# Starting rounds of the attention items inside a two-directional scan: (2, 8, 13, 20) becomes (1, 7, 12, 18)

## The chip, the cores and the metric

The kernel runs on one core of a Trainium2 chip. The metric is device time in microseconds (us) of one execution, lower is better. The engines that matter here are TensorE (PE, with its weight loads PEld), VectorE (DVE), ScalarE (ACT), GpSimd (POOL) and SyncE (SP), which issues most DMAs.

## The reference, cut to what matters

The program is two blocks of a model in a row. Each of the two layers of the first block computes, for 1040 tokens, a latent attention of 4 heads and a gated linear recurrence of 8 heads that runs forwards and backwards; both read the same projection and do not depend on each other. Their outputs are concatenated, projected, normalised, and sent through a mixture of experts. The second block (differential attention, gated MLP, feed-forward) comes after and is not touched.

```
y_att = _mla(c_q, c_kv, k_pe, ...)            # softmax(q k^T) v, 4 heads
y_f = _wkv_scan(rh, decay, kd, vh, kk, a, reverse=False)   # S = S*w - sa*b + v*k, step by step
y_b = _wkv_scan(rh, decay, kd, vh, kk, a, reverse=True)
mixed = concatenate([y_att, y_rwkv]) @ w_out[li]
```

## The kernel before, in words

All five engines run an instruction order written out by hand; semaphores tie them together, and each engine takes its instructions strictly as they are written.

**The scan.** In each layer the recurrence is cut into 10 steps of 104 tokens for each direction d (0 forwards, 1 backwards). A step is 32 phases in 23 rounds (`PHASES`, `STEPS` = 23). Direction 1 runs 11 rounds behind direction 0 (`STAGGER`), so that while one direction prepares a step the other solves and puts out its own. A round is numbered 0 to 22 after direction 0. Direction 0 is in phases 0 to 2 in round 0, 3 to 5 in round 1, 6 to 10 in round 2, 11 in round 3, 12 in round 4, 13 and 14 in round 5, 15 in round 6, and then one phase a round; direction 1 does the same from round 11 on. I call round 0 to 10 the first half of a step (direction 0 prepares) and round 11 to 22 the second half (direction 1 prepares).

- Phase 0 is a product with `u` on PE (tiles `u,w` and `u,a`). Phases 1 to 10 are element-wise work: DVE takes the product out of PSUM, ACT does two tanh, DVE a prefix sum (L1542) and the differences (L1548, L1555), ACT three exponentials (L1486, L1488, L1491: `ei`, `eK`, `ea`) and four scalings (L1495), DVE the scaled keys (L1568 `kr`, L1564 `hb`, L1571).
- Phase 11 transposes on PE (`consts,u`, `consts,hb`); it waits for `kr` of L1568. ACT takes the result out as `vT` (L1475), and phase 12 on PE waits for that. Phase 13 waits for L1580 on DVE, which takes phase 12 out.
- Phases 16 to 25 are five levels of a triangular inverse, each with two PE blocks (`T,lm`, then `XX,T` and `T,XX`); after each block DVE (L1600, L1608), and after the second one ACT too, must empty the bank before the next block of the same direction can start. Phases 26 to 31 put out the state and the outputs (`S,kr`, `rh,T`, `vT,hbT` and others).

**The attention** of a layer is 40 items (4 heads by 10 tiles of 104 tokens) in the first layer and 32 (4 by 8 tiles of 128) in the second. An item takes six rounds, k = 0 to 5:

- k = 0: PE, two thirds of the scores (10 matmuls, `kn,qn` and `kpe,...`); k = 1: PE, the last third (5 matmuls), and on DVE the row maximum (L1826 three times, L1829, L1831)
- k = 2: ACT, three exponentials with sums (L1811); SP loads the query of the item after the next one
- k = 3: PE, nine transposes (`consts,p`), and DVE (L1843) and ACT (L1798) copies of them
- k = 4: PE, the product with the values (`v,pT`, 18 matmuls)
- k = 5: DVE scales the output (L1851), ACT squares it (L1815), SP stores it

In every round each engine's order is: one direction, then the attention, then the other direction. The direction in phases 0 to 11 (its first four rounds) always comes last; else direction 0 comes first.

**Where an item begins** is what the change touches. `item_starts` takes four rounds a step (`STARTS`) in the first layer, and in steps 0 and 5 of the second; the other steps of the second layer take three (`FEWER`). The first place is left out in step 0. Nothing else in the schedule moves.

Of the kernel before, what the change touches and what calls it, by code (L numbers as in the profile page):

```python
# [1675 lines left out]

STARTS = (2, 8, 13, 20)
FEWER = (2, 9, 17)  # L1680


def item_starts(li):

    made = []
    for q in range(NT + 1):
        places = STARTS if li == 0 or q in (0, 5) else FEWER
        made += [STEPS * q + at for at in places if q or at != STARTS[0]]
    return made[:4 * TILES_OF[li]]
# [2700 lines left out]
```

## Time and profile before

| what | value |
|---|---|
| median of three runs | 4875.96 us (4870.5 to 4881.09) |
| the profiled execution | 4875.28 us, its span 4873.4 us |
| mean granted clock of TensorE | 0.959 |
| busy over the span | PE 91%, PEld 78%, DVE 64%, ACT 44%, POOL 24% |
| scan and attention of the first layer | 357.0 to 1097.7 us: 740.7 us |
| scan and attention of the second layer | 2174.6 to 2896.9 us: 722.3 us |

The profile is of one execution. Times in it count from the first instruction. A row of the timeline gives start, length, engine, line, operation, tiles and number of instructions, and in brackets the idle time before and what ended it. A helper issues most matmuls, so their line is L291; the tiles tell them apart. A row of the windows gives start and end, length, then for PE, PEld, DVE, ACT and POOL the busy time and the number of instructions, then TensorE's granted clock, the share of DMA time and GB/s. The start of one block on PE to the start of the next is what the block costs PE, since the last matmul of a block still drains while the next ones run.

### The profile page before, as it was taken

What the parts mean: (1) busy time and instruction counts of PE and PEld (TensorE: products, weight loads), DVE (VectorE), ACT (ScalarE), POOL (GpSimd) and SP (SyncE); (2) the same over time, 40 slices, a digit from 0 to 9 for tenths busy, and PEclk for the clock granted to TensorE, in tenths of its full rate; (3) what the DMA queues carried; (4) which work ended last, traced back from release to release, by engine and by line L of the source; (5) the groups of instructions that cost most, each with busy time, mean ns of one, the idle gap of its engine ahead of it and who ended that gap; (6) DMA issues with size and microseconds to landing.
All of it is one profiled execution on the core that took longest, in us unless ns stands there. A gap on an engine that the chain in (4) does not pass through costs nothing. (4 is left out here: it accounts for less than half of the span.)

```text
span 4873.4 us, 125669 instructions
## 1 busy us (share of the span) xinstructions
PE 4442.5 (91%) x55312; PEld 3786.9 (78%) x55312; DVE 3123.6 (64%) x4912; ACT 2158.3 (44%) x3962; POOL 1189.3 (24%) x863
## 2 busy tenths in 40 slices
PE   6989999989799969989989889899979979999999
PEld 6888888886588858878888877688857657888887
DVE  5436666669698874346666677898864475661752
ACT  2333444442388852434434341688743252331431
POOL 1003222322244520012322221444321001222221
PEclk9999999999799989999999999899989799999999
DMA  5411111133367664311111132576651003333332
GB/s 149 144 52 37 39 23 34 25 86 86 135 260 265 252 204 121 114 55 28 36 36 24 24 112 88 223 260 260 239 181 35 9 8 123 95 103 114 116 113 91
DMA packets 378339, 535.76 MB, mean 110 GB/s; under 512 B 117501, under 2 KB 301885, under 8 KB 349749
## 3 DMA queue, kind: packets, MB, share of 16 engines
q1 hardware_dynamic: 335701, 488.54, 30.9%
q0 software_dynamic: 40752, 33.95, 2.3%
q8 instruction: 439, 7.19, 0.6%
q10 hardware_dynamic: 1344, 5.24, 0.3%
q14 instruction: 103, 0.84, 0.1%
HBM read 569.43 MB, written 121.40 MB: 142 GB/s over the span
## 5 line engine op out<-in xcount | busy, mean ns | idle before, releaser
L291 PE MATMUL ps<-w_hi,xbT 128*128 128x512 f32 x1520 | 499.9, 400 | 19.7 <-DVE w L2839 19.7
L291 PE MATMUL ps<-hT,w_in 128*128 128x416 f32 (+1 forms) x2736 | 496.2, 340 | 4.1 <-DVE hT L3126 4.1
L291 PEld LDWEIGHTS ps<-hT,w_in 128*128 128x128 f32 x2736 | 459.9, 196 | 30.3 <-issue 19.4
L2839 DVE TENSOR_TENSOR w<-w,w_hi 128x2048 fp32r<-128x2048 f32 x190 | 425.4, 2278 | 2.2 <-ACT w_hi L2796 2.2
L291 PEld LDWEIGHTS ps<-w_hi,xbT 128*128 128x128 f32 x1520 | 289.2, 190 | 87.5 <-DVE w L2839 28.7
L1657 POOL TENSOR_TENSOR lm<-Ab,consts 116x416 f32<-116x416 f32 x240 | 255.5, 1072 | 415.6 <-PE ps L291 245.2
L2796 ACT ACTIVATE w_hi<-w 128x2048 fp32r<-128x2048 f32 x190 | 355.2, 1935 | 0.0
L291 PE MATMUL ps<-w,xbT 128*128 128x512 f32 x760 | 299.3, 394 | 0.0
L2870 DVE TENSOR_TENSOR w<-w,w_hi 128x2048 fp32r<-128x2048 f32 x95 | 221.6, 2333 | 95.5 <-ACT w_hi L2832 95.5
L291 PE MATMUL ps<-w_hi,actT 128*128 128x512 f32 x760 | 250.8, 391 | 4.9 <-DVE actT L2865 4.9
L291 PE MATMUL ps<-x1T,w_gate 128*128 128x512 f32 x1056 | 248.4, 391 | 3.1 <-DVE x1T L3813 1.6
L291 PE MATMUL ps<-x1T,w_up 128*128 128x512 f32 x1056 | 246.5, 389 | 0.0
L291 PE MATMUL ps<-w_down,act 128*128 128x512 f32 x1056 | 241.3, 391 | 3.2 <-POOL w_down L4039 3.2
L1600 DVE TENSOR_TENSOR XX<-ps,consts 116x416 f32<-116x416 f32 x200 | 117.4, 587 | 193.4 <-PE ps L291 193.0
L291 PEld LDWEIGHTS ps<-x1T,w_gate 128*128 128x128 f32 x1056 | 199.4, 189 | 45.3 <-issue 1.9
L291 PEld LDWEIGHTS ps<-w_down,act 128*128 128x128 f32 x1056 | 199.2, 189 | 44.9 <-POOL w_down L4039 3.6
L291 PEld LDWEIGHTS ps<-x1T,w_up 128*128 128x128 f32 x1056 | 198.3, 188 | 41.1
L4030 POOL TENSOR_TENSOR w_up<-w_up,w_up 128x1024 fp32r<-128x1024 f32 x44 | 116.4, 2646 | 459.4 <-ACT w_up L3952 459.4
L291 PE MATMUL ps<-w_out,mixT 128*104 128x512 f32 (+1 forms) x864 | 218.8, 407 | 10.4 <-DVE w_out L2177 5.8
L2785 POOL DMA_INDIRECT t_ys<-yo,slots x95 | 101.3, 1066 | 464.4 <-PE ps L298 374.0
L291 PEld LDWEIGHTS ps<-w_out,mixT 128*104 128x104 f32 (+1 forms) x864 | 152.3, 179 | 67.4 <-DVE w_out L2177 9.5
L794 POOL TENSOR_TENSOR w_in<-w_in,w_in 128x1024 fp32r<-128x1024 f32 x22 | 56.0, 2546 | 604.8 <-ACT w_in L809 604.8
(464 smaller groups left out, 10782.1 us busy)
## 6 DMA issues: line engine op xcount, KB each, us to landing
w<-in_moe_w_dram SPq DMA_DIRECT2D x192, 1024.0 KB, 12.4
w_gate<-in_w_gate_dram SPq DMA_DIRECT2D x44, 512.0 KB, 3.9
w_up<-in_w_up_dram SPq DMA_DIRECT2D x44, 512.0 KB, 3.9
w_down<-in_w_down_dram SPq DMA_DIRECT2D x44, 512.0 KB, 3.6
w_in<-in_w_in_dram SPq DMA_DIRECT2D x36, 512.0 KB, 4.4
w_out<-in_w_out_dram SPq DMA_DIRECT2D x24, 512.0 KB, 7.7
t_h<-x SPq DMA_DIRECT2D x20, 416.0 KB
kn<-t_kn SPq DMA_DIRECT2D x8, 1040.0 KB, 5.2
```

What stands on the lines that cost most here:

```text
L291: made = e.matmul(out, a, b, start=start, stop=stop)
L794: e.tensor_tensor(w.lo, w.x, w.hf, ALU.subtract).then_inc(*count.tick(li, "lo", n))
L1600: e.tensor_tensor(m.XX[0:HP].rearrange("p (k u) t -> p k u t", k=2), both_banks(P, d, 0)[0:HP].rearrange("p k (u t) -> p k u t", t=H), bc( ...
L1657: e.tensor_tensor(m.LM[lv % 2][0:HP], m.ab[0:HP, :, 0, :], bc(m.lmask[0:HP, H * lv:H * lv + H].unsqueeze(1), [HP, 8, H]), ALU.mult).then_i ...
L2785: e.indirect_dma_start(T["ys"], bass.IndirectOffsetOnAxis(P.slots[:, table_column(b - 2):table_column(b - 2) + 1], 0), m.yo[b % 2], None, ...
L2796: e.activation(w.hi, w.x, ACT.Copy).then_inc(*P.c("moe_act").tick(li, "w13", b, k))
L2839: e.tensor_tensor(w.lo, w.x, w.hf, ALU.subtract).then_inc(*P.c("moe_dve").tick(li, "w13", b, k))
L2870: e.tensor_tensor(w.lo, w.x, w.hf, ALU.subtract).then_inc(*dv.tick(li, "w2", b))
L4030: e.tensor_tensor(w.lo, w.x, w.hf, ALU.subtract).then_inc(*po.tick(0, c, "lo", f))
```

## The change

The rounds in which items begin are other ones: each of the four places of a step is one round earlier, the last one two; of the three places, the first is one round earlier, the second two, and the third one later.

```
-STARTS = (2, 8, 13, 20)
-FEWER = (2, 9, 17)
+STARTS = (1, 7, 12, 18)
+FEWER = (1, 7, 18)
```

So with four places PE's attention blocks stand as follows (an item that begins late in a step ends in the next one):

| round | 0 | 1 | 2 | 3 | 4 | 5 | 6 | 7 | 8 | 9 | 10 | 11 | 12 | 13 | 14 | 15 | 16 | 17 | 18 | 19 | 20 | 21 | 22 |
|---|---|---|---|---|---|---|---|---|---|---|---|---|---|---|---|---|---|---|---|---|---|---|---|
| before, k | 3 | 4 | 0 | 1 | - | 3 | 4 | - | 0 | 1 | - | 3 | 4 | 0 | 1 | - | 3 | 4 | - | - | 0 | 1 | - |
| after, k | - | 0 | 1 | - | 3 | 4 | - | 0 | 1 | - | 3 | 4 | 0 | 1 | - | 3 | 4 | - | 0 | 1 | - | 3 | 4 |

## Rows read from the trace of the kernel before

**Rows 1.** Windows: a step of the first layer, a three-item step of the second.
```profile
564.02:634.62 70.60, 67.43 (x2009) 61.30 (x2009) 45.56 (x114) 30.24 (x86) 20.38 (x20) 1.00 0.12 24
2375.52:2445.07 69.55, 62.68 (x1975) 56.88 (x1967) 44.99 (x102) 28.10 (x77) 20.13 (x20) 1.00 0.11 23
```

**Rows 2.** Windows: the same step of the first layer in nine stretches.
```profile
564.02:572.51 8.49, 8.01 (x178) 7.06 (x177) 6.93 (x18) 3.92 (x10) 2.62 (x3) 1.00 0.22 48
572.51:588.18 15.67, 14.96 (x417) 13.87 (x419) 10.96 (x27) 6.83 (x21) 6.63 (x6) 1.00 0.09 19
588.18:596.58 8.40, 8.23 (x313) 7.51 (x310) 3.69 (x9) 3.78 (x11) 1.08 (x1) 1.00 0.14 29
596.58:598.11 1.53, 1.53 (x50) 1.34 (x46) 0.77 (x4) 0.38 (x1) 0.00 (x0) 1.00 0.01 1
598.11:606.60 8.49, 8.39 (x211) 7.44 (x210) 6.93 (x18) 3.81 (x10) 2.64 (x3) 1.00 0.17 35
606.60:611.91 5.31, 5.31 (x170) 5.00 (x170) 5.24 (x13) 4.67 (x15) 1.87 (x2) 1.00 0.21 38
611.91:620.24 8.33, 7.93 (x204) 7.09 (x203) 4.53 (x13) 1.99 (x6) 3.30 (x4) 1.00 0.02 4
620.24:631.87 11.63, 10.91 (x421) 10.15 (x415) 5.72 (x13) 3.42 (x11) 2.25 (x3) 1.00 0.04 9
631.87:634.62 2.75, 2.16 (x73) 1.84 (x74) 0.79 (x4) 1.43 (x5) 0.00 (x0) 1.00 0.24 53
```

**Rows 3.** Timeline of PE, same step: attention blocks and two waits.
```profile
565.63 2.21 PE L291 MATMUL ps<-v,pT 116*104 116x128 f32 x18
567.77 0.60 PE L291 MATMUL ps<-XX,T 52*52 52x52 f32 x32
...
568.70 0.72 PE L291 MATMUL ps<-kn,qn 128*104 128x348 f32 x3
...
570.45 0.60 PE L291 MATMUL ps<-T,lm 52*52 52x52 f32 x32
...
572.51 1.10 PE L291 MATMUL ps<-consts,u 64*52 64x64 f32 x32 [0.48 <-DVE kr L1568]
...
577.10 1.63 PE L291 MATMUL ps<-kr,hb 64*52 64x104 f32 x32 [0.59 <-DVE Ab L1580]
...
597.16 1.02 PE L298 MATMUL ps<-consts,p 104*116 104x104 f32 x9
```

**Rows 4.** Timeline of DVE, same step: the scaled keys and the row maximum.
```profile
569.71 0.58 DVE L1608 COPY T<-ps 116x416 f32<-116x416 f32 x1
...
571.87 0.59 DVE L1568 TENSOR_TENSOR kr<-kk,ps 128x416 f32<-128x416 f32 x1 [1.11 <-ACT ps L1488]
...
574.21 1.36 DVE L1826 TENSOR_REDUCE stat<-ps 104x1 f32<-104x348 f32 x3
...
575.87 0.58 DVE L1574 TENSOR_TENSOR hb<-aa,ei 128x416 f32<-128x416 f32 x1
```

**Rows 5.** Timeline of ACT, same step: squaring, first exponential, softmax.
```profile
570.59 0.31 ACT L1815 ACTIVATE pT<-o 104x128 f32<-104x128 f32 x1 [1.23 <-DVE o L1851]
...
570.90 0.53 ACT L1486 ACTIVATE ei<-cs 128x416 f32<-128x416 f32 x1
...
575.99 0.55 ACT L1811 ACTIVATE p<-ps,stat 104x348 f32<-104x348 f32 x1 [0.74 <-DVE stat L1831]
```

**Rows 6.** Windows: preparation stretches and first half, three-item step, second layer.
```profile
2375.52:2383.48 7.96, 5.99 (x168) 5.17 (x160) 6.92 (x16) 4.24 (x10) 2.62 (x3) 1.00 0.17 38
2375.52:2408.77 33.25, 29.56 (x888) 26.76 (x882) 22.08 (x50) 12.83 (x33) 10.03 (x10) 1.00 0.10 22
2409.51:2418.22 8.71, 7.06 (x203) 6.21 (x203) 7.62 (x19) 5.13 (x14) 2.63 (x3) 1.00 0.26 55
```

**Rows 7.** Windows: an idle PE late in the first scan, and what follows.
```profile
1052.80:1055.56 2.76, 0.03 (x4) 0.02 (x4) 0.00 (x0) 0.37 (x1) 0.00 (x0) 1.00 0.87 246
1055.90:1059.30 3.40, 3.40 (x81) 3.26 (x73) 2.40 (x5) 0.90 (x2) 0.00 (x0) 0.51 0.06 17
```

## The prediction

> **What bounds the kernel now.** The page says PE is busiest, but an average over many stages says little; the change touches the two scans alone, so I cut those into steps. In a step of the first layer PE is busy 67.4 of 70.6 us, in a three-item step of the second 62.7 of 69.55, at full clock [rows 1]. So PE sets the pace, with gaps. Those gaps decide here: the change adds and removes no instruction, it moves PE's attention blocks, and a block is free where PE would wait anyway and costs its length elsewhere.
>
> Next come nine stretches of one step, cut at PE blocks [rows 2]: from the product with `u` (phase 0) to the transposes of phase 11 (8.49); on to round 8 (15.67); to round 11 (8.40); the second half likewise, 1.53 up to direction 1's product with `u`, 8.49 to its phase 11, 5.31 to its phase 13, 8.33 to round 19, 11.63 to round 0, 2.75 to the next product with `u`. The two stretches of 8.49 I call the preparation. Phases 1 to 10 lie there: ten element-wise steps in a row on DVE and ACT while the preparing direction has nothing for PE. The wait that ends last says so: the transposes wait 0.48 us for `kr` of L1568, and that one waits for ACT's exponential L1488 [rows 3, 4].
>
> How long the preparation is without much attention, the second layer shows: 7.96 us with k = 0 and 1 alone inside [rows 6]. So it has a floor near 8 us, whatever PE has to do. The scan's own PE work in it is about 3.1 us, by the blocks that remain when attention is taken out. Some 4.9 us are free there, the largest free room in a step. The schedule of before puts k = 4, 0 and 1 into it: 2.14 + 1.75 + 0.9 = 4.8 us (start to start of blocks; k = 1 is five matmuls to the ten of k = 0) [rows 3], in both halves. It is nearly filled.
>
> **The change part by part**, for a four-item step. A block's price: k = 0 1.75, k = 1 0.9, k = 3 0.95 (597.16 to 598.11), k = 4 2.14 [rows 2, 3].
>
> *Preparation, first half (8.49).* It keeps k = 0 (round 1) and k = 1 (round 2) and loses k = 4, which now comes after, in round 5. Its length hardly falls. On the one side k = 5 leaves round 2: L1815 had stood in front of the first exponential, which began only at 570.90 [rows 5]. On the other the row maximum enters round 2 and stands on DVE ahead of `kr`, which is queued behind it in the same round. DVE's copy L1608 begins 5.69 us after the stretch (569.71), the maximum can begin 0.5 later, takes 1.66 (574.21 to 575.87), three tiny instructions 0.2, so `kr` begins at 8.06 and PE 0.64 later (571.87 to 572.51): 8.70 [rows 2 to 4]. Bounds: 7.96 [rows 6], and 9.4 if the maximum also starts late. I take 8.70, from the chain's own rows.
>
> *To round 8 (15.67).* k = 0 comes in (+1.75); k = 3 moves in front of the wait for L1580 and fills it (-0.59) [rows 3]; k = 4 in round 5 instead of 6 uncovers 0.15 behind phase 15, while k = 0 covers 0.2 in round 7. The softmax now runs in round 3 on ACT, 1.7 us (three of the kind at 575.99) [rows 5], ahead of `vT`, for which phase 12 waits: +0.4, bounds 0 and 1.1. Sum 17.2.
>
> *To round 11 (8.40).* k = 0 out, k = 3 in, and the softmax in round 9 ahead of ACT's copies: -1.75 + 0.95 + 0.3 = 7.9.
>
> First half: 32.56 becomes 33.8, **+1.2**.
>
> *Second half.* 1.53 becomes 2.7: k = 4 in place of k = 3, in front of the product with `u`, where nothing waits. Preparation: as above, plus DVE's L1851 (k = 5 is in round 12 here) and a later start of the maximum, 9.05. To phase 13: k = 4 is added, 5.31 + 2.14 - 0.1 = 7.35. To round 19: k = 0 for k = 4, and a wait of 0.4 goes (PE is busy 7.93 of 8.33): 7.55. To round 0: k = 1, 3 and 4 for 0 and 1, +1.34, and the softmax in round 20 makes the transposes and two level blocks wait, +0.95 (bounds 0 and 1.7): 13.9. The last one loses k = 3: 1.8. 38.04 becomes 42.35, **+4.3** [rows 2].
>
> Together +5.5 us a step. The added waits (0.15, 0.4, 0.3, 0.95) are counted as if no other wait took them up, so I halve them: **+4.6**. Bounds: 1.9 (no added wait, both preparations about 8 us) and 7.3.
>
> *Three-item steps.* First half: preparation 7.96 to 8.7, then the same moves, 33.25 to 34.2. Second half (36.30, the rest of 69.55 [rows 1, 6]): before, k = 3 and 4 lie in the preparation, which takes 8.71 [rows 6]; after, nothing does, and it takes 7.75 (8.71 less the copies of k = 3 on DVE and the waits they made). Those 3.3 us go to rounds 10, 11, 21 and 22, while k = 0 and 1 cover some waits in rounds 18 and 19: 37.6. Together +2.2, bounds 0 and 4.
>
> PE then idles about 3.2 us in one piece in each of these second halves: the level block of round 13 must be emptied by DVE, where L1540 to L1555 of direction 1 stand ahead of it, and no attention lies between. In this trace an idle stretch of 2.76 us was followed by 3.4 us at a granted clock of 0.51, the lower of the two levels (1.2 GHz) [rows 7]. At half speed 3.4 us of PE hold 1.7 us of work; part waits for DVE anyway, so I take +0.8, bounds 0 and 3.4. The Trainium skill, TensorE: Matmul & The Clock Gate, section "Why this matters for your kernels", asks for no long idle gap between bursts of matmuls, since the clock falls back after one; the trace agrees.
>
> *DMAs.* Query loads and stores move with their items on SP's queue; a query is loaded some ten rounds ahead, and POOL has no attention work. In the last step the store of k = 5 in round 17 comes ahead of the loads for the closing stage; these are used three rounds later, so I take 0, at most 4 us a layer.
>
> **Sum.** First layer: nine steps from 1 to 9 by 4.6, 41; the first step's second half +3, the last rounds, whose items end earlier, -3: 41. Second layer: one four-item step 4.6, the first step +3, eight three-item steps by 3.0, 24: 32. Together +73 on 4875.3, the profiled execution, which is 0.7 us under the median: **4948 us** (+1.5%). About 0.2%, 10 us, can be told from no change.
>
> **The rivals.**
>
> *The clock falls in the first layer too.* After the change PE does only 0.5 us of work in the last 3.2 us of the preparation of the first half. For it: rows 7. Against it: the longest idle piece there is 1.75 us by my reckoning. If it falls, 19 halves lose up to 1.7 us each, about +40: 4988. Chance 0.12.
>
> *The moved blocks are hidden anyway.* PE's busy time counts matmuls that overlap; weight loads are busy only 61.3 of 70.6 us [rows 1], so up to 9 us a step might be room in which k = 4 sinks. Against it: at the new places of k = 4 (rounds 11 and 22) the blocks before and after follow one another without a recorded gap, and round 22's wait comes behind it. Then +0: 4875. Chance 0.06. The Trainium skill, Perfetto Trace Analysis, "Identifying the Most-Contended Engine", says that matmul busy time is no measure of headroom and weight loads are; by that rule the step has 13% of room, and the sum would be this rival's.
>
> *Faster: the chain, not the cover, decides.* If PE has room, a step is as long as the preparing direction's chain, and the change shortens it: k = 5 no longer delays the first exponential (8.49 to 7.96 in both halves, 1.06), and k = 3 fills the wait for L1580 (0.59). That is 1.65 a step, 19 steps in all: 4844. It decides if the transposes of phase 11 begin less than 8.0 us after the product with `u` and 1.53 does not grow with k = 4. Against it: the maximum stands ahead of `kr`. Chance 0.11.
>
> **How the numbers follow.** My forecast has 0.71. Its own range, from the bounds (1.9 to 7.3 for 11 steps or so, 0 to 4 for eight, the clock 0 to 3.4), is not likely at its ends at once: 4892 to 5000. To hold 8 in 10 I reach to the clock's case: 4885 to 5005, which leaves the two lower rivals and little more out. Slower 0.83, same 0.06, faster 0.11.
>
> **What would show it.** Right: in the first layer the preparation stays between 8 and 9.2 us while PE is busy there some 2 us less, and `kr` begins right behind L1831 instead of behind ACT; the wait for L1580 is gone; the stretch before direction 1's product with `u` is 2.7. In the second layer PE idles about 3 us before `XX,T` in round 14, then runs below full clock. Wrong: preparations under 8 us, a step of 70.6 or less, or k = 4 in rounds 11 and 22 taking up waits that I took for work.

## The result and the profile after

| kernel | median, us | against before |
|---|---|---|
| before, in the same runs | 4878.52 (4870.50 to 4886.76) | |
| after | 4997.88 (4996.05 to 5008.86) | 1.0256, interval 1.0241 to 1.0272 |

The change makes the kernel slower by 2.6%. The profiled execution took 4998.44 us (span 4996.5, mean granted clock 0.945). Measured on PE from the first to the last block of scan or attention (some 3 us more than the stretches in the table of before), the first layer went from 743.4 to 808.2 us and the second from 725.2 to 781.8: +64.8 and +56.6, which is the whole difference but for 2 us.

First the windows of after, in the columns of rows 2: a step of the first layer, its nine stretches cut at the same PE blocks, and the time around a fall of the clock; then a three-item step of the second layer, its first preparation, and the time around a fall of the clock there.

```profile
587.53:666.83 79.30, 72.13 (x2015) 65.25 (x2008) 46.65 (x112) 30.17 (x86) 21.56 (x20) 0.94 0.09 21
587.53:596.21 8.68, 5.93 (x166) 5.09 (x160) 8.15 (x21) 5.37 (x14) 2.61 (x3) 0.97 0.17 36
596.21:614.32 18.11, 18.11 (x428) 16.60 (x430) 9.87 (x22) 5.43 (x18) 7.10 (x6) 0.92 0.03 7
614.32:622.44 8.12, 7.76 (x311) 6.99 (x308) 4.73 (x13) 4.10 (x12) 1.07 (x1) 1.00 0.13 28
622.44:625.17 2.73, 2.73 (x60) 2.53 (x56) 0.59 (x1) 0.38 (x1) 0.00 (x0) 1.00 0.09 20
625.17:634.18 9.01, 6.32 (x193) 5.43 (x192) 7.63 (x20) 4.62 (x13) 2.64 (x3) 0.94 0.23 48
634.18:644.23 10.05, 10.05 (x188) 9.57 (x188) 5.36 (x13) 4.06 (x13) 4.59 (x4) 0.71 0.01 2
644.23:651.92 7.69, 7.44 (x196) 6.56 (x196) 3.27 (x7) 1.79 (x6) 1.41 (x2) 1.00 0.04 11
651.92:665.91 13.99, 12.87 (x448) 11.61 (x436) 7.04 (x17) 4.42 (x13) 2.14 (x2) 1.00 0.11 24
665.91:666.83 0.92, 0.92 (x64) 0.86 (x64) 0.00 (x0) 0.00 (x0) 0.00 (x0) 1.00 0.27 58
592.85:595.60 2.75, 0.61 (x33) 0.51 (x32) 2.68 (x11) 2.27 (x6) 0.22 (x1) 1.00 0.26 58
595.60:599.00 3.40, 2.79 (x52) 2.79 (x54) 3.27 (x7) 2.80 (x9) 1.84 (x2) 0.50 0.06 13
...
2535.65:2610.98 75.33, 66.61 (x1974) 60.78 (x1967) 44.79 (x102) 28.05 (x77) 20.29 (x20) 0.93 0.09 21
2535.65:2544.33 8.68, 6.00 (x167) 5.17 (x160) 8.15 (x21) 5.37 (x14) 2.62 (x3) 1.00 0.19 43
2575.40:2578.70 3.30, 1.06 (x72) 0.81 (x60) 3.20 (x8) 1.74 (x5) 1.89 (x3) 1.00 0.17 40
2578.80:2585.60 6.80, 5.22 (x150) 5.23 (x154) 3.78 (x10) 4.02 (x10) 1.69 (x2) 0.50 0.02 3
```

Against [rows 2] the nine stretches read as follows.

| stretch | before | predicted | after |
|---|---|---|---|
| preparation, direction 0 | 8.49 | 8.70 | 8.68 |
| to round 8 | 15.67 | 17.2 | 18.11, clock 0.92 |
| to round 11 | 8.40 | 7.9 | 8.12 |
| to direction 1's product with `u` | 1.53 | 2.7 | 2.73 |
| preparation, direction 1 | 8.49 | 9.05 | 9.01 |
| to its phase 13 | 5.31 | 7.35 | 10.05, clock 0.71 |
| to round 19 | 8.33 | 7.55 | 7.69 |
| to round 0 | 11.63 | 13.9 | 13.99 |
| to the next product with `u` | 2.75 | 1.8 | 0.92 |
| step | 70.60 | 76.1 | 79.30 |

The preparations last as long as predicted while PE is busy 2.1 us less in them. Two stretches are longer than predicted, by 0.9 and 2.7 us, and those two are the ones with the lowest clock, 0.92 and 0.71. In the two preparations the fall lies only in the last us (0.97 and 0.94), where PE idles and does not lose by it. The last stretch is 0.9 shorter. Before, no step from 1 to 8 of the first layer had a stretch at half speed; after, there are 13 in these steps, and 14 in the same steps of the second layer, each 3.4 or 6.8 us long. The 13 begin about 1 us or less before or after the transposes of phase 11 begin, at 13 of 16 preparations. Three timelines of after, at the end of a preparation of direction 0, show how that looks. PE:

```profile
593.95 0.60 PE L291 MATMUL ps<-T,lm 52*52 52x52 f32 x32 [1.09 <-ACT ei L1486]
596.21 1.95 PE L291 MATMUL ps<-consts,u 64*52 64x64 f32 x32 [1.66 <-DVE kr L1568]
```

DVE:

```profile
593.22 0.58 DVE L1608 COPY T<-ps 116x416 f32<-116x416 f32 x1
593.72 1.36 DVE L1826 TENSOR_REDUCE stat<-ps 104x1 f32<-104x348 f32 x3
...
595.30 0.15 DVE L1831 TENSOR_SCALAR stat<-stat 104x1 f32<-104x1 f32 x1
...
595.58 0.58 DVE L1568 TENSOR_TENSOR kr<-kk,ps 128x416 f32<-128x416 f32 x1
```

ACT:

```profile
593.79 0.50 ACT L1488 ACTIVATE ps<-x 128x416 f32<-128x416 f32 x1
...
596.12 0.53 ACT L1811 ACTIVATE p<-ps,stat 104x348 f32<-104x348 f32 x1
...
598.21 0.60 ACT L1475 ACTIVATE vT<-ps 116x512 f32<-116x512 f32 x1 [0.41 <-PE ps L291]
```

`kr` no longer waits for ACT as in [rows 4]; it stands right behind the row maximum, and begins 1.29 us after the exponential that it needs (L1488) has ended. PE idles 1.09 us, does one level block of 0.60, idles 1.66, and the transposes of phase 11, 1.10 us before [rows 3], take 1.95.

### The profile page after: what moved, and what is told of

It is laid out like the page before. It is cut to its first block and busy times, and to the rows that moved or that the text cites. A ratio compares the mean times of both kernels' runs of the same rounds, so it can differ in the third digit from the quotient of the medians.

```text
span 4996.5 us, 125669 instructions
## 1 busy us (share of the span) xinstructions
PE 4512.8 (90%) x55312; PEld 3842.6 (77%) x55312; DVE 3126.1 (63%) x4912; ACT 2154.1 (43%) x3962; POOL 1203.3 (24%) x863
```

## The experiments

The state of the theories at the start: theory A says that room in the preparations was lost (two blocks k = 4 a step now stand where PE does not wait) and that the clock falls on top; rival B that the queues do it (the row maximum ahead of `kr` on DVE, the softmax ahead of `vT` on ACT); rival C the clock alone. All results in one table; steps are means over steps 1 to 8 (second layer: without the four-item step), "half" counts the stretches at half speed in these steps of the two layers.

| kernel | median, us | ratio to before, interval | step, layers 1 and 2 | half |
|---|---|---|---|---|
| before | 4876.97 to 4880.55 in three groups of runs | 1 | 71.4, 69.9 | 0, 0 |
| after | 4997.88 | 1.0256, 1.0241 to 1.0272 | 78.9, 75.3 | 13, 14 |
| PE kept busy | 4958.39 | 1.0160, 1.0135 to 1.0186 | 76.5, 73.2 | 1, 0 |
| order turned on both | 4945.45 | 1.0140, 1.0111 to 1.0169 | 75.5, 73.0 | 1, 7 |
| before without two k = 4 | 4880.78 | one run | 71.9, 69.8 | 1, 1 |
| after without two k = 4 | 4971.57 | one run | 75.5, 75.2 | 12, 15 |
| both repairs | 4953.51 | 1.0159, 1.0142 to 1.0176 | 76.8, 73.0 | 0, 0 |
| both, without two k = 4 | 4923.68 | 1.0097, 1.0080 to 1.0114 | 73.8, 72.4 | 1, 0 |
| order turned on DVE alone | 5004.64 | 1.0273, 1.0255 to 1.0290 | 79.2, 75.5 | 7, 12 |
| order turned on ACT alone | 5015.25 | 1.0272, 1.0253 to 1.0291 | 79.9, 75.8 | 9, 15 |
| first half's places alone | 4926.35 | 1.0109, 1.0092 to 1.0126 | 76.4, 69.5 | 9, 1 |
| before, order turned | 4865.25 | 0.9962, 0.9948 to 0.9976 | 70.2, 69.6 | 0, 1 |
| before, second layer 2, 13, 20 | 4888.34 | 1.0016, 1.0006 to 1.0027 | 71.6, 70.0 | 0, 2 |

**PE kept busy.** The changed kernel, with PE multiplying constants in the emptied rounds, so that it idles less there.

```
+AWAKE = {2: 2, 3: 3, 13: 2, 14: 2}
+AWAKE3 = {2: 2, 3: 3, 13: 5, 14: 1}
+def stay_awake(e, P, li, n):
...
+    mms(e, [(P.ps[7][:, 256:512], P.K["ident"], P.cr[:, 0:256], True, True)] * times)
...
             att_pe(e, P, li, n)
+            stay_awake(e, P, li, n)
```

> The changed kernel, with extra matmuls on constants (into an unused part of bank 7) in rounds 2, 3, 13 and 14 of steps 1 to 9, where PE idles during the preparation; they add nothing to the outputs. Theory A, the lost room (k = 4 left the preparation and costs its length elsewhere, and on top of it the clock falls in the idle preparation): the half-speed stretches go, which is about 2.5 us a step of the first layer and 2.5 to 3 of the second, 40 to 60 us in all: 4940 to 4955 us; steps of the first layer fall from 79 to about 76.5. Rival B, the queues (the row maximum ahead of kr and the softmax ahead of vT are what costs): within 20 us of the changed kernel, 4980 or more. Rival C, the clock alone: most of the 120 us comes back, under 4910.

Measured: 39.5 us under after, 3 us above the range of A and far from C. Its windows of the step that was shown above, both preparations, the stretch to phase 13, the step, and the stretch to round 8:

```profile
577.49:586.16 8.67, 8.31 (x176) 6.86 (x169) 8.14 (x21) 5.36 (x14) 2.62 (x3) 1.00 0.18 37
614.19:623.13 8.94, 8.24 (x201) 6.82 (x200) 7.56 (x20) 4.62 (x13) 2.65 (x3) 1.00 0.23 47
623.13:630.48 7.35, 7.35 (x188) 6.97 (x188) 5.19 (x13) 3.84 (x13) 4.09 (x4) 1.00 0.02 4
577.49:653.07 75.58, 72.44 (x2034) 64.43 (x2027) 46.41 (x112) 29.83 (x86) 21.57 (x20) 1.00 0.11 22
586.16:603.20 17.04, 16.81 (x428) 15.37 (x430) 9.88 (x22) 5.30 (x18) 7.12 (x6) 1.00 0.03 7
```

The added matmuls lengthen no preparation (8.67 and 8.94 against 8.68 and 9.01), and at full clock the stretch to phase 13 takes 7.35, where the prediction had 7.35, and the one to round 8 17.04 for 17.2. The trace of after bears that out without any added matmul: of its second halves in steps 1 to 8, the one in which the clock did not fall has 7.35 to phase 13, the seven others 8.66 to 10.12. So the difference is close to the price of the clock: 2.4 us a step in the first layer (78.9 to 76.5) and 2.1 in the second. The other 5.1 and 3.3 us a step are not the clock.

**Order turned on both.** In rounds 2 and 13 DVE, in rounds 3 and 14 ACT does the preparing direction ahead of the attention.

```
+def lead_first(places):
+    for n, parts in groupby(rounds(), key=lambda x: x[0]):
+        parts = list(parts)
+        if n % STEPS in places:
+            parts.sort(key=lambda x: x[1] is None)
+        yield from parts
...
-    for n, parts in groupby(rounds(), key=lambda x: x[0]):
+    for n, parts in groupby(lead_first((3, 14)), key=lambda x: x[0]):
...
-    for n, part in rounds():
+    for n, part in lead_first((2, 13)):
```

> The changed kernel, but in rounds 2 and 13 DVE does the preparing direction before the attention (kr before the row maximum), and in rounds 3 and 14 ACT does it before the softmax (vT before the exponentials). Theory A, the lost room: the preparation falls from 8.7 and 9.0 us to about 8.0 and 8.2, and the wait for vT goes; with the clock better or not, 10 to 45 us less: 4955 to 4985. Rival B, the queues: what stood in front was the whole cost, so 80 us or more come back, under 4920. Rival C, the clock alone: PE idles about as long as before in the preparation, so nearly nothing: 4990 or more.

Measured: 52 us under after, 10 us below the range of A and 25 above that of B. Its windows: both preparations, to phase 13, the step.

```profile
576.31:583.75 7.44, 5.93 (x168) 5.08 (x160) 6.66 (x16) 4.13 (x10) 2.62 (x3) 1.00 0.17 34
611.64:619.34 7.70, 6.32 (x192) 5.43 (x191) 6.06 (x15) 3.38 (x9) 2.64 (x3) 1.00 0.24 47
619.34:628.25 8.91, 7.65 (x188) 7.13 (x188) 6.78 (x18) 5.21 (x16) 3.45 (x4) 1.00 0.06 10
576.31:651.15 74.84, 68.72 (x2016) 61.52 (x2008) 45.92 (x112) 30.10 (x86) 20.07 (x20) 1.00 0.11 22
```

The preparations fall by 1.24 and 1.31 us, so the row maximum had cost that much in each, and with the shorter preparations the clock stays up in the first layer. But the stretch to phase 13 is 8.91, not 7.35. PE and DVE in it:

```profile
622.60 0.65 PE L291 MATMUL ps<-T,lm 52*52 52x52 f32 x32 [1.26 <-DVE T L1608]
623.18 1.04 PE L298 MATMUL ps<-consts,p 104*116 104x104 f32 x9
```

```profile
620.21 1.36 DVE L1826 TENSOR_REDUCE stat<-ps 104x1 f32<-104x348 f32 x3
...
621.87 0.58 DVE L1608 COPY T<-ps 116x416 f32<-116x416 f32 x1
```

The row maximum, moved behind `kr`, now stands right ahead of DVE's copy L1608, and the level block of round 14 waits 1.26 us for that copy; k = 3 follows without a wait. So 1.5 of the 2.55 us that the two preparations gave are lost again. The queues are a part of the loss, not the whole.

**Two blocks k = 4 left out, before and after.** The blocks that stand in the preparations before are those of items that begin in rounds 8 and 20; the same two, of rounds 7 and 18, stand outside after.

```
+            last = 0 if li == 0 and ITEM_STARTS[li][item] % STEPS in (8, 20) else NKT - 1
...
-                    for j, n in ((j, min(KT, L - KT * j)) for j in range(NKT))])
+                    for j, n in ((j, min(KT, L - KT * j)) for j in range(last + 1))])
```

> The kernel of before, leaving out in the first layer 8 of the 9 matmul pairs of k = 4 for the items that begin in rounds 8 and 20, that is the two k = 4 blocks that lie in the preparations (1.9 us of PE work each, so about 3.8 us a step; these items' outputs are only part sums). Theory A, the lost room: those blocks are free where they stand, so the two preparations stay near 8.5 us and a step of the first layer stays within 1 us of 71. If k = 4 costs its length wherever it stands, the step falls by 3.8 us and the time by 36. Rival C, the clock alone: the emptier preparation lets the clock fall, steps grow by 1 to 3 us.

> The changed kernel, leaving out the same matmuls of k = 4 in the first layer for the items that begin in rounds 7 and 18; these blocks now stand in rounds 11 and 22, outside the preparations (these items' outputs are only part sums). Theory A, the lost room: the blocks cost their length there, so a step of the first layer falls by 3.5 to 3.8 us, 79 to about 75.3, and the time by 33 to 37 us. Rivals B and C: the blocks hide behind the waits, the step falls by less than 1 us.

Measured: nothing (4880.78 against 4880.55) where they stood before, 26 us where they stand after, for the 33 to 37 expected; a first-layer step falls from 78.9 to 75.5. These are single runs, but the four of after lie within 13 us. What is left out is eight ninths of two blocks of 2.14, 3.8 us: at the new places they cost nearly their length (3.3 us a step, with 12 falls of the clock for 13), at the old ones nothing. This shows the lost room directly. It also ends the rival that the moved blocks are hidden. The reading that this rival took from the Trainium skill, Perfetto Trace Analysis, section "Identifying the Most-Contended Engine", that headroom on TensorE is judged by weight loads and not by matmuls, fails here where it is taken over a whole step: by it these blocks had 9 us to sink into [rows 1], and the runs show hardly any of that at the new places. Taken by stretch it comes nearer: before, weight loads were busy 1.34 of 1.53 us in one of the two stretches that took a k = 4, and 10.15 of 11.63 in the other [rows 2].

The first of these two kernels shows one thing more. Windows of a preparation, and of its last 2.75 us:

```profile
567.54:576.03 8.49, 6.39 (x162) 5.33 (x161) 6.93 (x18) 3.92 (x10) 2.63 (x3) 1.00 0.24 51
573.28:576.03 2.75, 1.57 (x37) 1.23 (x37) 1.64 (x8) 1.92 (x6) 0.00 (x0) 1.00 0.12 27
```

It is nearly as empty as that of after (6.39 against 5.93 us busy), yet the clock fell once in these eight steps, and not behind a preparation. Here k = 1 stands at its end, in round 3; after, k = 1 is over in round 2, and of the last 2.75 us PE works 0.60.

**Both repairs together.**

```
             att_pe(e, P, li, n)
+            stay_awake(e, P, li, n)
...
-    for n, part in rounds():
+    for n, part in lead_first((2, 13)):
```

> The changed kernel with both repairs at once: DVE and ACT do the preparing direction ahead of the attention (rounds 2, 13 and 3, 14), and PE multiplies constants in the emptied preparations. Theory A now (three separate losses: k = 4 laid outside the preparations, the queue in front of kr and vT, the clock): what is left is the lost room alone. The order alone left 65 us, of which some 15 are half-speed stretches that it left in the second layer; so 4925 to 4938. Rival B (the reordering helped only through the clock, by making the idle pieces shorter; the queues themselves cost nothing): with the clock held up in both, nothing is gained on the better of the two, 4943 to 4958. Rival D (the added matmuls are themselves in the way once the preparation is short): slower than the order alone, over 4948.

Measured: no better than either repair alone, so the number of theory A was wrong. The preparation of this kernel takes 8.45 us in the median, against 7.44 with the order alone: once the chain is short, the constant matmuls are in its way, as rival D says. The number alone would fit rival B as well (4943 to 4958). But the queues did cost something with the clock held up: with the order alone the preparation was 1.24 us shorter at 1.00, and here it is still 0.2 us shorter than with PE kept busy alone. The repairs cannot be added up.

**Both repairs, without the two k = 4.**

```
+            last = 0 if li == 0 and ITEM_STARTS[li][item] % STEPS in (7, 18) else NKT - 1
```

> As the one with both repairs, and without 8 of the 9 matmul pairs of k = 4 for first-layer items that begin in rounds 7 and 18 (their outputs are left incomplete): the two blocks that left the preparations. Theory A: nothing of the first layer's loss is left, its scan takes 735 to 752 us (before: 743, after: 808), and the whole is 25 to 35 us under the kernel with both repairs, 4895 to 4910. If something unnamed costs time as well (softmax against the levels of the inverse, transfers), the first layer's scan stays above 757 us, less than 18 us under the kernel with both repairs.

Measured: 30 us under both repairs, as expected, but 14 us above the range for the whole, and the first layer's scan takes 764.5 us, not 735 to 752. So 21 us were still unnamed; the windows of direction 1 (preparation, then to phase 13) and two rows of PE name most of it:

```profile
605.62:614.66 9.04, 8.38 (x201) 6.82 (x200) 7.38 (x18) 4.36 (x12) 2.65 (x3) 1.00 0.26 52
614.66:623.45 8.79, 8.06 (x188) 7.09 (x188) 6.05 (x17) 4.45 (x14) 3.84 (x4) 1.00 0.01 3
```

```profile
617.04 0.60 PE L291 MATMUL ps<-T,lm 52*52 52x52 f32 x32 [0.39 <-DVE T L1608]
617.88 1.54 PE L298 MATMUL ps<-consts,p 104*116 104x104 f32 x9 [0.23 <-ACT p L1827]
```

8.79 against 7.35 in the kernel without the turned order. The level block waits for L1608 again, and k = 3, which stands ahead of phase 12, waits for the softmax (L1827 here), which starts later; k = 3 then takes 1.54 us for 1.02 [rows 3]. These 1.4 us a step, or 13 us in nine steps, are a cost of the repair. The rest, some 8 us, stays unnamed.

**The order turned on one engine alone.** First on DVE (`kr` ahead of the row maximum), then on ACT (`vT` ahead of the softmax): each is one of the two changed loops above.

```
-    for n, part in rounds():
+    for n, part in lead_first((2, 13)):
```

> The changed kernel with the order turned on DVE alone (rounds 2 and 13: kr ahead of the row maximum); ACT still does the softmax ahead of vT. Theory A: the preparation shrinks by some 0.5 us in both halves and the clock stays up in part of the first layer; the phases after it wait longer for vT, since the softmax begins later. 4955 to 4972 (after: 4998, both orders turned: 4945). If the row maximum is the whole of the queue's cost: 4940 to 4952. If the softmax is: 4980 or more.

```
-    for n, parts in groupby(rounds(), key=lambda x: x[0]):
+    for n, parts in groupby(lead_first((3, 14)), key=lambda x: x[0]):
```

> The changed kernel with the order turned on ACT alone (rounds 3 and 14: vT ahead of the softmax); DVE still does the row maximum ahead of kr. Turned on DVE alone, it gained nothing: the preparation fell to 7.44, but phase 12 then waited 4.98 us behind phase 11 for vT, which stood behind a softmax that began later. Theory A (the two queues hand the delay to each other; only both turned help): the preparation stays 8.7, the step from phase 11 to 12 falls from 2.6 to 1.9 to 2.2 in the first half, and grows in the second, where k = 3 waits for the softmax; the clock still falls in most preparations. 4985 to 5005. Rival (the softmax ahead of vT is the queue that costs): 4945 to 4965.

Measured: neither gains anything; each alone is at least as slow as after. The first lies where the softmax alone was to cost, but not for that reason, as the second shows; the second is 10 us over the top of theory A's range. With DVE alone turned, ACT and then PE in the same preparation as above:

```profile
597.81 0.55 ACT L1811 ACTIVATE p<-ps,stat 104x348 f32<-104x348 f32 x1 [1.39 <-DVE stat L1831]
...
599.40 0.60 ACT L1475 ACTIVATE vT<-ps 116x512 f32<-116x512 f32 x1
```

```profile
595.16 1.10 PE L291 MATMUL ps<-consts,u 64*52 64x64 f32 x32 [0.41 <-DVE kr L1568]
...
600.14 1.10 PE L291 MATMUL ps<-kr,hb 64*52 64x104 f32 x20 [2.98 <-ACT vT L1475]
```

`kr` is early, but the maximum behind it is late, ACT waits 1.39 us for it at the head of its queue, and `vT`, whose input has long been there, waits behind three exponentials. The delay was handed from one queue to the next. With ACT alone turned the preparation stays at 8.69, since `kr` is as late as in after, and in the second half PE waits at k = 3:

```profile
635.63 1.54 PE L298 MATMUL ps<-consts,p 104*116 104x104 f32 x9 [0.84 <-ACT p L1811]
```

**The first half's places alone.** Before, with the first two of the four places moved.

```
-STARTS = (2, 8, 13, 20)
+STARTS = (1, 7, 13, 20)
```

> Before, with two of the four places of the first layer moved: (1, 7, 13, 20), the three-item steps as before. It parts room from queue: the first half keeps k = 4, 0 and 1 in its preparation and gets the row maximum ahead of kr and the softmax ahead of vT; the second half loses k = 4 from its preparation and gets no queue. Theory A: the second half grows by 1.5 to 2.2 us, the first by 0.2 to 1, together +18 to +30: 4898 to 4912, and up to 15 more if the clock falls in the second halves. Rival B (queue first): the first half grows by over 2 us and the second by less than 0.5.

Measured: +49 us, with all of it in the first half: 35.0 to 40.7 us in the mean, and the second half from 36.4 to 35.7. Theory A gave 4898 to 4912, and its 15 more were for a clock that falls in the second halves; all nine falls lie in the first. By the numbers this is what rival B asked for. The windows (preparation, to direction 1's `u`, its preparation, second half), DVE and ACT in the first preparation, and PE at its end show why:

```profile
576.06:587.05 10.99, 7.86 (x178) 7.15 (x178) 8.69 (x23) 3.92 (x10) 2.60 (x3) 1.00 0.19 41
587.05:616.54 29.49, 28.52 (x782) 26.07 (x782) 15.82 (x36) 10.95 (x34) 7.45 (x7) 0.94 0.08 17
616.54:625.04 8.50, 6.30 (x192) 5.42 (x192) 6.87 (x16) 4.13 (x11) 2.66 (x3) 1.00 0.14 29
616.54:651.93 35.39, 32.34 (x1051) 29.37 (x1050) 22.58 (x56) 15.06 (x43) 10.09 (x10) 1.00 0.09 20
```

```profile
582.98 1.36 DVE L1826 TENSOR_REDUCE stat<-ps 104x1 f32<-104x348 f32 x3
...
584.74 0.35 DVE L1851 TENSOR_SCALAR o<-ps,stat 104x128 f32<-104x128 f32 x1
```

```profile
585.13 0.31 ACT L1815 ACTIVATE pT<-o 104x128 f32<-104x128 f32 x1 [2.14 <-DVE o L1851]
...
585.44 0.53 ACT L1486 ACTIVATE ei<-cs 128x416 f32<-128x416 f32 x1
```

```profile
587.05 1.42 PE L291 MATMUL ps<-consts,u 64*52 64x64 f32 x32 [3.13 <-DVE kr L1568]
```

The expectation had two faults. The block k = 4 that leaves direction 1's preparation goes to round 11, ahead of direction 1's `u`, so its 2.14 us are paid in the first half; and the second preparation, emptied to 6.30 us, stays at 8.50, so nothing comes back for it. And in round 2 k = 5 of one item now meets the maximum of the next: L1851 stands behind the maximum, L1815 waits for it, and the first exponential stands behind L1815. Every link of the preparation's chain from there on is late, and it takes 10.99 us. PE idles 3.13 us in one piece at its end, and the clock fell at the end of all eight such preparations. So this run parts room from queue only in that both are seen to cost; their sizes here are not those of the change.

This kernel has the closest match to the emptied preparation of after. Its second preparations are as empty (6.30 us busy, against 6.32 for direction 1 after), but PE works 1.88 of their last 2.75 us, against 0.99; the clock fell at none of the eight, and at seven of the eight after.

**Before, with the order turned.** In rounds 2 and 13 DVE and ACT do the preparing direction first, so that k = 5 no longer stands ahead of the exponentials; the places are those of before.

```
-    for n, parts in groupby(rounds(), key=lambda x: x[0]):
+    for n, parts in groupby(lead_first((2, 13)), key=lambda x: x[0]):
...
-    for n, part in rounds():
+    for n, part in lead_first((2, 13)):
```

> The kernel before with DVE and ACT doing the preparing direction ahead of the attention in rounds 2 and 13 (k = 5 and its squaring no longer stand ahead of the exponentials). Theory A (in the first layer PE fills 8.0 of the preparation's 8.49, so a shorter chain has 0.5 us to give): first layer 0 to 0.5 us a preparation, second layer, three-item steps, about 0; 4865 to 4878. Rival (chain, not cover, decides there as well): the preparations fall to 7.5 in the first layer, 4855 to 4862.

Measured: 13.4 us faster, 0.4%, at the lower end of theory A's range, and the fastest kernel here. Windows of a preparation and of a step:

```profile
562.42:570.35 7.93, 7.93 (x178) 7.06 (x177) 7.14 (x18) 4.12 (x10) 2.61 (x3) 1.00 0.20 40
562.42:631.47 69.05, 66.81 (x2010) 61.11 (x2009) 46.36 (x114) 30.69 (x86) 20.07 (x20) 1.00 0.12 24
```

The chain is shorter, and the preparation stops at PE's own 7.93 us of work: it is full. In the median the first preparation falls from 8.49 to 7.94 us and the second to 8.33. A queue's order is worth 0.6 and 0.2 us here, where the room is used, and 1.24 and 1.31 where it was given up.

**The second layer's places at 2, 13 and 20.**

```
-FEWER = (2, 9, 17)
+FEWER = (2, 13, 20)
```

> The kernel before with the three places of the second layer at 2, 13 and 20, so that a three-item step is a first-layer step without the item of round 8: k = 4, 0 and 1 in the first preparation, 0 and 1 in the second. By the first layer's stages (a step of 71.3 without k = 0, 1 and 3 of that item, 1.75, 0.9 and 0.95, its k = 4 being free) a step takes 67.0 to 68.5 against 69.6: 8 steps, -9 to -20 us, 4857 to 4868. Rival (the waits in the emptied rounds come up, or the clock falls in the long half without attention): 4872 to 4895.

Measured: 0.2% slower, so the rival was right. A three-item step takes 70.0 us in the mean; two of the seven take 68.4 and less, the others 70.0 to 71.2. That the room of the preparations is fuller was not enough; which waits came up in the emptied rounds was not followed further.

## Why the prediction was right in direction and too small

The direction, the range (4885 to 5005) and the mechanism of the forecast held: 4998 against 4948. Of +121 us in the two scans it had 73.

*What bounds the kernel, and the free room:* right. Two blocks k = 4 cost nothing in the preparations and nearly their length outside.

*The stretches:* right to 0.15 us in both preparations, in the one of 2.7, and in those to rounds 19 and 0; 0.2 too low to round 11; right at full clock for those to round 8 (17.04 for 17.2) and to phase 13 (7.35). The wait for L1580 at phase 13 went as said, and `kr` stands behind L1831. Too high by 0.9 was the last one (0.92 for 1.8): before, PE idled 0.59 us of it [rows 2], and that left with k = 3.

*Halving the added waits (+5.5 to +4.6):* with the clock held up the step shown takes 75.58 for the 76.1 of the hand sum; over the mean of the steps the cost is 5.1, between the two. So the halving took off some 0.5 us a step too much, 4 us in all.

*The clock:* this is the step that failed. The prediction kept it at full speed in the first layer, since "the longest idle piece there is 1.75 us by my reckoning", and gave the other case 0.12. The longest piece is 1.66, close to that, and the clock falls all the same, at 13 of 16 preparations; in the second layer it falls at seven of the eight first preparations too, where the sum had it in second halves alone. That is worth 2.4 us a step in the first layer and 2.1 in the three-item steps, where the sum had 0 and 0.8: some 28 of the missing 48 us. The rival's 4988 is the case that came nearest, though its price does not follow from its own terms: 19 halves by 1.7 us are 32 and not 40, which gives 4980. The Trainium skill, TensorE: Matmul & The Clock Gate, section "Why this matters for your kernels", warns of long idle gaps between bursts; read as a rule on single gaps it does not bear on the first layer, and the trace shows falls there with a block of 0.60 us between two idle pieces.

*Three-item steps:* 2.2 without the clock were 3.3, another 8 us over seven steps. PE idled 2.67 us ahead of `XX,T` in round 14, for the 3.2 reckoned, and the second preparation takes 8.01 in the median, for 7.75. Which stretch has the rest was not taken apart.

*The edges:* the first steps cost 6.4 and 6.6 us for 3 each, the ends -1.3 and +5.5 for -3 and 0, together 14 us more; a four-item step of the second layer 6.3 for 4.6; against that, nine and eight steps were counted where eight and seven are whole, 8 us too much.

*Rivals:* "hidden anyway" fell with the left-out blocks. "The chain decides" fell in its own place, since the preparation did not get shorter; but its mechanism is real: turned loose from the places, in the kernel before with the order turned, a shorter chain is worth 13 us. No run tests the DMAs, which the sum put at nothing.

## What to carry to other kernels

A block of work moved out of a stretch that waits for other engines can cost nearly its full length at the new place and give nothing back at the old one, as here, so price both places, and do it by leaving the block out. Ask next where in the emptied stretch the idle time now lies: in these runs preparations with work at their end kept TensorE's clock up, and most of those as empty with idle time there did not. These kernels differ in more than that, so the cause is likely and not shown by itself. When an engine's queue holds a chain up, turn the order on every engine that the chain runs through, since one alone gained nothing here, and look at what the moved work then stands in front of.

## Unexpected in the hardware

The granted clock fell from 1.00 to 0.50, the lower of its two levels (1.2 GHz), after 2.75 us in which PE did 0.61 us of work in the first layer (1.06 us in 3.30 in the second), with no idle piece over 1.66 us in the first, and stayed there for 3.40 or 6.80 us. It does not fall each time: the three preparations of the first layer at which it stayed at 1.00 are as empty as the others, with the same idle pieces. After 2.75 us with 1.57 or 1.88 us of work, in two other kernels, it stayed at 1.00 at all of eight. In the stretch at half speed the 32 transposes of phase 11 took 1.95 us for 1.10.
